# A hybrid decoder step: two loads change places, gates become column strips, one copy moves ahead of a scale

## The reference, cut to what matters

```python
o_hg, s_hg = hgrn2_mixer(q, f, i, g, lb, hg_norm, s0)   # s0: the sample sequences' states
o_cmp, o_slc = nsa_cmp_slc(q, pos, cmp_rows, slc_rows, ...)
g = sigmoid(ngate).reshape(B, L, 3, NSA_HEADS, 1)       # the branch gates, 24 columns of h @ w_in
o_nsa = g[:, :, 0] * o_cmp + g[:, :, 1] * o_slc + g[:, :, 2] * o_win
mg = sigmoid(mgate).reshape(B, L, 2, D_MODEL)           # the merge gates, 2048 columns of h @ w_in
merged = mg[:, :, 0] * (o_hg @ W_a) + mg[:, :, 1] * (o_nsa @ W_b)
x = x + merged @ w_out
```

## Time and profile before

| what | value |
|---|---|
| median of 3 runs | 1176.08 us |
| the three runs | 1176.12, 1176.08 and 1165.91 us |
| the profiled execution, whole | 1166.02 us |
| its span, first to last instruction | 1164.2 us |
| its mean granted clock of PE | 0.996 of 2.4 GHz |
| PE busy | 1142.0 us, 98% of the span |
| PE's share of the chain that ended last | 94% |

### The profile page before, as it was taken

How to read it: one execution, slowest core, us unless ns; L and a number is a source line. 1 busy time by engine, 2 the same in 40 slices (tenths; PEclk the granted TensorE clock), 3 DMA queues, 4 the chain that set the end, 5 groups by cost and what they waited for, 6 DMA issues and landing times.

```text
span 1164.2 us, 21121 instructions
## 1 busy us (share of the span) xinstructions
PE 1142.0 (98%) x8613; PEld 1032.4 (89%) x8613; DVE 707.1 (61%) x1302; ACT 544.1 (47%) x867; POOL 173.2 (15%) x300
## 2 busy tenths in 40 slices
PE   6999999999999999999999999999999999999997
PEld 5987776778999999999999787676899999999997
DVE  5686265457567777763558644545756677776442
ACT  4532275653355555542454234755435555554231
POOL 1154300013110100100105450000312110010000
PEclk9999999999999999999999999999999999999998
DMA  9555332347644444324456525213784444432501
GB/s 292 164 150 190 107 99 73 109 119 219 223 153 134 158 157 155 123 93 160 145 133 212 165 86 167 73 40 119 220 266 154 137 157 151 145 109 91 178 29 46
DMA packets 151498, 165.99 MB, mean 143 GB/s; under 512 B 31492, under 2 KB 114214, under 8 KB 151078
## 3 DMA queue, kind: packets, MB, share of 16 engines
q1 hardware_dynamic: 151402, 164.64, 45.3%
HBM read 156.22 MB, written 12.46 MB: 145 GB/s over the span
## 4 chain that ended last, share of the span: by engine, by line
PE 94%; DVE 2%; DMA 1%; ACT 1%; issue 0%; SPq 0%; DVEq 0%; ACTq 0%
PE mm L671 66%; PE ax L671 23%; PE ax L674 5%; DMA ring<-in_state_hgrn 1%; ACT mixb L1325 1%; DMA attb<-in_norm_final 0%; DVE ring_low L1681 0%; DVE mixb L1831 0%; DVE mixb L2096 0%; DVE work_parts L2065 0%; PE mm L674 0%; DVE mixb L1848 0%; DVE mixb L2097 0%; DVE merged_low L2065 0%; DVE mixb L2250 0%
## 5 line engine op out<-in xcount | busy, mean ns | idle before, releaser
L671 PE MATMUL mm<-work_parts 128*128 128x320 f32 (+2 forms) x1120 | 356.5, 318 | 1.1 <-DVE h_low L1675 1.1
L1681 DVE TENSOR_TENSOR ring_low<-ring,work_parts 128x2048 fp32r<-128x2048 f32 (+2 forms) x116 | 256.0, 2207 | 125.4 <-ACT work_parts L1325 124.7
L671 PE MATMUL mm<-h_low,work_parts 128*128 128x320 f32 x1024 | 319.3, 312 | 0.0
L671 PE MATMUL mm<-work_parts,ring_low 128*128 128x320 f32 x1024 | 315.6, 308 | 0.0
L1325 ACT ACTIVATE work_parts<-ring 128x2048 fp32r<-128x2048 f32 (+2 forms) x116 | 211.9, 1827 | 159.7 <-PE mm L671 90.3
L671 PEld LDWEIGHTS mm<-work_parts 128*128 128x128 f32 (+1 forms) x1120 | 209.2, 187 | 9.2 <-issue 2.0
L671 PEld LDWEIGHTS mm<-h_low,work_parts 128*128 128x128 f32 x1024 | 193.0, 188 | 0.3
L671 PEld LDWEIGHTS mm<-work_parts,ring_low 128*128 128x128 f32 x1024 | 193.1, 189 | 0.0
L671 PE MATMUL ax<-act_parts,work_parts 128*128 128x320 f32 x544 | 127.2, 312 | 0.6 <-DVE ring L2087 0.6
L671 PE MATMUL mm<-act_parts,work_parts 128*128 128x320 f32 x480 | 117.4, 310 | 0.3 <-DVE merged_low L2065 0.3
L671 PE MATMUL mm<-hT,ring 128*128 128x320 f32 x384 | 109.6, 437 | 0.0
(11 more groups left out here) (235 smaller groups left out, 1584.7 us busy)
## 6 DMA issues: line engine op xcount, KB each, us to landing
ring<-in_w_gate_up SPq DMA_DIRECT2D x44, 1024.0 KB, 7.0
ring<-in_w_in SPq DMA_DIRECT2D x10, 2048.0 KB, 8.5
ring<-in_w_in SPq DMA_DIRECT2D x18, 1024.0 KB, 5.7
ring<-in_w_down SPq DMA_DIRECT2D x8, 1536.0 KB, 6.7
ring<-in_w_out SPq DMA_DIRECT2D x4, 2048.0 KB, 13.9
ring<-in_w_down SPq DMA_DIRECT2D x4, 2048.0 KB, 8.1
ring<-in_w_in SPq DMA_DIRECT2D x32, 128.0 KB, 3.1
ring<-in_cache_cmp_kv SPq DMA_DIRECT2D x32, 128.0 KB
```

The lines of the kernel that those rows point to most:

```text
L671: return nc.tensor.matmul(out, lhsT, rhs, start=start, stop=stop)
L1681: V.tensor_tensor(unit_of(u, ring_r), unit_of(u, ring), unit_high(u).bitcast(F32), ALU.subtract).then_inc(*st.up(w_low[l]))
```

## The change

Three edits, in both layers. First, `st1` and `mg2` change places in `BLOCKS`: `st1` becomes number 15, loaded after `ov5`, and `mg2` becomes number 16, loaded after `mgb3`; in SP's list the stores of `st1` now stand ahead of the load of `br1` and of the wait for `mg2`'s last use. Second, the prompt's branch gates are no longer made by `compressed_rows`. A new PE step `prompt_gates` holds 32 columns of the weights still (8 of values and 24 of gates) and moves all 256 prompt tokens, four k-tiles side by side in four strips of 32 output rows; ACT copies the bank to `gtF`; a second step `prompt_gates_turned` turns it over and adds the four strips by two products with a constant `gsum` (four shifted identities, built by three additions on DVE at the start); ACT takes one sigmoid of 48 columns. Each bank plan gets one entry more. Third, on DVE `unit_turned(0)` stands ahead of `unit_scale(1)`.

```diff
@@ -65,7 +65,7 @@


 BLOCKS = (["par", "w_hf", "w_hq", "w_nq", "cmp", "w_hi", "w_kvn", "w_kvc", "w_cmp", "w_hg", "mg0", "kv0", "mg1", "kv1",
-           "st0", "mg2", "st1", "br0", "mg3", "br1", "wo0", "wo1"] + [f"ff{n}" for n in range(NJ // JPB)]
+           "st0", "st1", "mg2", "br0", "mg3", "br1", "wo0", "wo1"] + [f"ff{n}" for n in range(NJ // JPB)]
           + [f"dn{mh}_{n}" for mh in range(2) for n in range(len(DOWN[mh]))])
 NBLK = len(BLOCKS)
 assert NBLK % NSLOT == 0
@@ -114,7 +114,8 @@

 def mm_plan():
     out = [("par", "V")] + [(f"hf{h}", "V") for h in range(HH)] + [(f"hq{h}", "V") for h in range(HH)]
-    out += [(f"nq{m}", "V") for m in range(4)] + [(f"{x}{i}", "A") for x in ("hi", "kvn", "kvc") for i in range(3)]
+    out += [(f"nq{m}", "V") for m in range(4)] + [(f"{x}{i}", "A") for x in ("hi", "kvn") for i in range(3)]
+    out += [("kvc0", "A"), ("kvc1", "A"), ("gtf", "A"), ("kvc2", "A")]
     out += [(f"hg{h}", "V") for h in range(HH)]
     for m in range(KD):
         out += [(f"mga{m}", "A"), (f"mgb{m}", "A")]
@@ -129,7 +130,7 @@
     out += level_plan(0) + level_plan(1) + level_plan(2) + [(f"cc{s}", "A") for s in range(4)]
     out += level_plan(3) + level_plan(4) + level_plan(5) + level_plan(6) + [(f"cc{s}", "A") for s in range(4, NSEQ)]
     out += [(f"nqr{m}", "V") for m in range(4)] + [("kt0", "A"), ("kt1", "V")]
-    out += [("cp", "A"), ("hidk", "A"), ("hidv", "A"), ("gsel0", "V"), ("gsel1", "V")]
+    out += [("cp", "A"), ("gtt", "A"), ("hidk", "A"), ("hidv", "A"), ("gsel0", "V"), ("gsel1", "V")]
     out += [("kcm", "A")] + [(f"vc{n}", "A") for n in range(3)] + [("kcr", "V")]
     out += [(f"krt{h}", "AV"[h % 2]) for h in range(HH)] + [("scc0", "V"), ("scc1", "V")]

@@ -265,6 +266,8 @@
         kcT = work[:, 4608:4608 + NCS * NCB].rearrange("p (s n) -> p s n", s=NCS)
         stok = work[:, 4744:6280].rearrange("p (i c) -> p i c", i=3)
         ctok = work[:, 6280:7048].rearrange("p (i c) -> p i c", i=3)
+        gtF = work[:, 7048:7048 + SEQ]
+        gsum = sb("gsum", 24)
         kvT = work[:, 7048:9096].rearrange("p (w b t) -> p w b t", w=2, b=4)
         gts = sb("gts", 3 * 24)[:, :].rearrange("p (i c) -> p i c", i=3)
         gsel = sb("gsel", 12)[:, :].rearrange("p (h c) -> p h c", h=2)
@@ -707,10 +710,24 @@
                         for g in range(2):
                             last = mm(bank[SMP * g:SMP * g + SMP, 0:140], hT[:, k, SEQ:T], w[:, k, 140 * g:140 * g + 140],
                                       k == 0, k == KD - 1)
-                for k in range(KD if i < 2 else 0):
-                    last = mm(bank[0:TM[i], 256:280], hT[:, k, P * i:P * i + TM[i]], w[:, k, 256:280], k == 0,
-                              k == KD - 1)
                 last.then_inc(mm_full[L], 1)
+
+            def prompt_gates():
+
+                w = kt_of("w_kvc", KD, 280)
+                bank = begin(MM[L], "gtf")
+                for k in range(KD):
+                    strip = slice(32 * (k % 4), 32 * (k % 4) + 32)
+                    last = mm(bank[strip, 0:SEQ], w[:, k, 248:280], hT[:, k, 0:SEQ], k < 4, k >= 4)
+                last.then_inc(mm_full[L], 1)
+
+            def prompt_gates_turned():
+
+                bank = begin(AXR[L], "gtt")
+                pe.wait_ge(*MM[L].emptied_at("gtf"))
+                for i in range(2):
+                    last = mm(bank[:, 24 * i:24 * i + 24], gtF[:, P * i:P * i + P], gsum[:, :], True, True)
+                last.then_inc(ax_full[L], 1)

             def feature_tile(name, w, cols, first=0, end=KD):

@@ -1096,6 +1113,7 @@
                     rows_turned(q)
                 compressed_rows(0, l)
                 compressed_rows(1, l)
+                prompt_gates()
                 for m in range(4):
                     bank = begin(AXR[L], f"nqr{m}")
                     pe.wait_ge(*MM[L].emptied_at(f"nq{m}"))
@@ -1109,6 +1127,7 @@
                     last.then_inc(ax_full[L], 1)
                 rows_turned(NSEQ)
                 compressed_rows(2, l)
+                prompt_gates_turned()

                 pe.wait_ge(*landed_at("w_cmp", l))
                 w1 = slot("w_cmp")[:, 0:2048].rearrange("p (v j e) -> p v j e", v=2, e=ND)
@@ -1417,7 +1436,6 @@
                 for i in range(3):
                     bank = take(MM[L], f"kvc{i}")
                     if i < 2:
-                        A(gts[:, i, :], bank[:, 256:280], ACT.Sigmoid)
                         A(ctok[:, i, :], bank[:, 0:256], ACT.Copy).then_inc(*st.up(mm_act[L]))
                     else:
                         A(gts[0:SMP, i, :], bank[SMP:P, 116:140], ACT.Sigmoid)
@@ -1426,10 +1444,16 @@
                     if i == 1:
                         sc.wait_ge(*st.settled())
                         pair_rows(NSEQ, ctok[:, 0:2, :])
+                        bank = take(MM[L], "gtf")
+                        A(gtF, bank[:, 0:SEQ], ACT.Copy).then_inc(*st.up(mm_act[L]))
                         bank = take(AXR[L], "kt0")
                         A(ktn[:, 0, :], bank[:, 0:T], ACT.Copy).then_inc(*st.up(ax_act[L]))
                         bank = take(AXR[L], "cp")
                         A(cmp_rows(NSEQ), cmp_bank(bank), ACT.Copy).then_inc(*st.up(ax_act[L]))
+
+                bank = take(AXR[L], "gtt")
+                A(gts[:, 0:2, :], bank[:, 0:48].rearrange("p (i c) -> p i c", i=2), ACT.Sigmoid).then_inc(
+                    *st.up(ax_act[L]))

                 take(AXR[L], "hidk")
                 bank = take(AXR[L], "hidv")
@@ -1701,6 +1725,9 @@
                 ve.wait_ge(*st.settled())


+            link(V.tensor_tensor(gsum[:, :], ident[:, 8:32], ident[:, 40:64], ALU.add))
+            link(V.tensor_tensor(gsum[:, :], gsum[:, :], ident[:, 72:96], ALU.add))
+            link(V.tensor_tensor(gsum[:, :], gsum[:, :], ident[:, 104:128], ALU.add))
             big = lbs[:, 0:4]
             link(V.tensor_tensor(big, pro[:, 0:4], pro[:, 4:8], ALU.max))
             link(V.tensor_tensor(lbs[:, 4:12].rearrange("p (l h) -> p l h", l=2),
@@ -1968,8 +1995,8 @@
                 compressed_scale()
                 unit_reduce(1)
                 unit_scale(0)
+                unit_turned(0)
                 unit_scale(1)
-                unit_turned(0)
                 unit_reduce(2)
                 unit_out(0)
                 out_gate(0)
```

## The result

The changed kernel takes 1181.99 us, the median of six runs (1179.99 to 1182.32). The six runs of the kernel before that stand beside them, three of which are the ones on which the forecast was put, have a median of 1172.19 us (1165.91 to 1176.12). The ratio is 1.0084, with a 95% interval of 1.006 to 1.0108: some 10 us slower, between 7 and 13, which is within the 1% that counts as no change here, though not zero. The profiled execution of the changed kernel has a span of 1179.0 us, 14.8 us above that of before; the one of before was among its fastest.

What follows compares the result with a forecast made beforehand. PE, busy 98% of the span, was taken to bound the kernel. Gates -4.0, blocks +6.2, clock +2.8 and copy -0.9 gave +4.1 us on the 1176.1 us median: 1180.2 us, range 1165 to 1186.

Steps and rivals of the forecast that it cites:

- The strips: Prompt gates on PE: 3.5 us removed, 1.0 for strip passes and 0.5 for turning added; net 2.0 us saved per layer.
- The rival without overlap: Gate strips run one after another: gates cost 1.2 us more a layer, 1186.6 us in all; chance 0.07.
- What hid the rest of part 1: ACT's copy to `gtF`, the later `kt0` and DVE's additions for `gsum` were to cost PE nothing.
- The load of `br1`: Issued 9 to 10 us later behind the `st1` stores, landing at 292 to 294, hidden by 3 to 5 us.
- The stall: PE ahead of `split_gates(4)`, waiting for `mg2` through load, ACT and DVE: 4.5 us where it stood 1.31.
- part 2: State block loaded ahead of the merge gates `mg2`: 3.2 and 3.0 us lost, 6.2 us in both layers.
- The clock behind the stall: One fall to 1.2 GHz per layer over twelve products, 1.4 us each, 2.8 us in all.
- the rival on the slow side: Clock stays down through state deltas and turned outputs, 8 us lost per layer: +17.3 us, 1193.4; chance 0.06.
- The sample for the clock: End of the old trace: after 24 one-column passes in 3.02 us, twelve products at 0.27 us each, granted clock 0.52.
- The turned copy: DVE's copy ahead of the scale of unit 1 spares PE's bank wait: 0.9 us gained in both layers.
- the prediction's own sign: Forecast wrong if PE's stall before the split gates is under 2 or over 7 us, or new waits stand elsewhere.
- Nothing in the change bears on that difference: Two of three timed runs lay 10.1 us above the profiled execution; this spread was held unrelated to the change.

Runs made afterwards that it cites:

- The filled stall: Changed kernel with ten unneeded products issued in PE's stall ahead of the first split gates: 1174.53 us, ratio 1.0032 to the kernel before.
- three pairs: Kernels with strips against without: strips alone and the kernel before; wait filled; wait filled and output gates spread. Time less clock cost: -2.9, -3.3, -2.8 us.
- strips with the early reduction: Kernel before with gates as strips, and the turned copy and the reduction of unit 2 ahead of the scale of unit 1: 1171.20 us, ratio 1.0017.
- the kernel before once more: The kernel before, unchanged, one further run for another look at its clock: 1169.07 us.
- the last one: Kernel before, no strips, with two unneeded products in the second state block's wait and output gates spread over the narrow stretches: 1165.61 us, ratio 0.9959.

## Why the prediction was right, and where its steps failed

The time was forecast at 1180.2 us and is 1182.0; "no change that can be told" was the likeliest case and came. That the two times lie so near is luck: two errors went opposite ways. The change costs about 9.8 us beside its own runs of before (7 to 13), not 4.1, and the base on which the 4.1 was put, 1176.1 us from three runs, was 4 us above the median of the six beside the change and 7 above that of 35 later ones. What was right is the mechanism of the main loss, the stall that DVE's low part of `mg2` ends and the fall of the clock with it. Step by step:

- **The strips: right.** They overlap as the sample scores did. The products fell by 2.5 us per layer, exactly 3.5 less 1.0; the turning cost 0.70 instead of 0.5. Net 1.8 for 2.0. The rival without overlap is out: the 16 passes took 1.07 us together. But the time doesn't show the saving, since the clock is lower with strips.
- **What hid the rest of part 1: right.** No new wait for `gtF`, `kt0` or `gsum` stands in PE's list.
- **The load of `br1`: hidden, as forecast, by other numbers.** It was issued at 289.87 us, 16.6 us later than before and not 9 to 10, and landed 5.6 to 9.2 us after its issue, not 10 to 11; ACT came to it only at 304.58.
- **The stall: right mechanism, a size off.** Load 8.2 us forecast, 8.3 measured; ACT 1.9, 1.91. The step that failed is "DVE's low part, 2.28 us": beside POOL's decays it took 3.65 and 3.54 us. PE began at 14.0 us after `mgb3` instead of 12.5, the stall is 6.14 us and not 4.5, and part 2 lost 9.6 us against the old waits (6.14 less 1.31 and 1.40) where 6.2 was said. The duration was taken from a place where POOL did nothing on that buffer, and moved to one where it did.
- **The clock behind the stall: right mechanism, a size off.** One fall per layer, as forecast, but 4.3 us in all on the split products (8.80 and 9.96 against 7.25 twice) and not 2.8: the fall lasted 6.8 and 10.2 us, where the sample at the end of the trace was taken as twelve products long. The filled stall separates it from the wait itself. The lasting fall, the rival on the slow side, did not come.
- **The sample for the clock: misread.** The forecast took the fall at the end of before for that of a weak, half idle stretch, and for a case of a PE that waits. It isn't: PE was busy for the whole of the 3.40 us ahead of it, the last 2.90 with passes of one column, and in the fall itself too:

```profile
1143.40:1146.80 3.40, 3.40 (x31) 3.28 (x30) 0.19 (x1) 0.46 (x1) 0.00 (x0) 1.00 0.02 5
```

So the forecast's remark that the trace agrees at its end doesn't hold for that row. It bore on the narrow passes of the compressed branch, to which the forecast didn't apply it. An idle PE at the lower clock stands in that trace only behind its last product, from 1157.0 us on (granted 0.53 and 0.50). That the clock would fall in the stall was right, but the sample did not speak for it.

- **The turned copy: wrong.** The forecast was a gain of 0.9 us "bounds 0 and 0.9", since PE's next use of the delayed scale was `turned(1)`. It looked at who needs the scale, and not at what stands behind the scale in DVE's queue: the reduction of unit 2, whose bank PE needs for `values(0)`, sooner than `turned(1)`. PE's waits there went from 0.9 to 1.8 us. By the prediction's own sign ("if new waits stand elsewhere") this step of the forecast is wrong.
- **"Nothing in the change bears on that difference": wrong.** The 10 us between the runs of before were set aside as not of the change. Part of that spread is the clock behind the wait for `st1`, which the change removes: with that wait filled the twelve runs of the kernel without strips lie between 1163.5 and 1170.0 us, the 23 of before beside them between 1165.9 and 1174.8. The spans of the two profiles differ by 14.8 us and the medians by 9.8; the kernel before pays in some executions what its profile doesn't show.
- **Not foreseen at all:** falls in the compressed branch, at narrow passes with a busy PE, some 4.7 us in the changed kernel's profile (12.07 and 12.09 against 10.40 twice, and about 1.4 us at 720 us). They come in the kernels with strips above all.

In the profiles: strips -5.0, turning +1.4, falls in the compressed branch +4.7, copy +0.8, stall +9.6, clock behind it +4.3, which is 15.8 us against 14.8 between the spans. Two more differences bring it to 15.2: the start takes 0.8 us more in the changed kernel, and it hasn't the fall of 1.4 us that the kernel before has at its end.

That the strips' work doesn't show in the time is thus settled as far as the clock goes: three pairs have it saved and lost again. Open is why the clock is lower with strips, and what decides whether a narrow stretch brings a fall in a given execution. A fall at the compressed branch costs 1.5 to 1.7 us by the chains shown (12.07 for 10.40, and 1.10 and 5.76 for 0.72 and 4.50), somewhat more than the 1.2 us of some expectations.

## What to carry to other kernels

When a transfer is moved, follow the whole path from landing to use, and take the duration of each step from a place with the same neighbours: DVE's 2.28 us became 3.65 beside POOL. When an instruction is moved forward in a queue, price its wait for every instruction behind it, down to the next bank that the bottleneck engine needs. And look at the spread of the runs before setting it aside: here it pointed at a short wait behind which the clock falls. Two products that nobody needs, put into that wait, gave 3.7 to 5.4 us in the kernel with strips, while the 3.6 us of real work that the strips removed never came through, because the clock fell with them. A saving on the busiest engine has to be weighed against its granted clock, over many runs.

## What the runs showed of the hardware

Behind a wait of PE of 1.82 us, in a stretch of narrow passes, the clock went to 1.2 GHz and stayed there for 10.2 us, although PE was busy all that time; it fell behind waits of 2.08 and 2.44 us at the same place too (strips with the early reduction, and the kernel before once more), and stayed at 2.4 GHz behind the seven of 1.22 to 1.55 us. A PE that is busy without a gap can still see the clock fall, where the passes are narrow (131 and 701 us of the changed kernel, 134 us of the last one). Replacing, in each of two layers, 32 passes of 24 columns by 16 strip passes and 4 short ones saved about 3 us at full clock and cost 2.8 to 5.2 us in clock. And DVE's subtraction of two tiles in SBUF lost nearly the whole time that POOL's product on SBUF tiles, started first, ran beside it (1.37 of 1.51 us, and the same in four other overlaps).
